# Two blocks on one core: factor transposes one product later in block one, both first low halves ahead of the upper transposes in block two

## The reference

```python
def reference(x, ...):
    x = first_block(x, ...)          # 2 layers
    return second_block(x, mem, ...) # 2 layers, then a last norm

# first_block, layer i
    xn = rmsnorm(h, norm_g[i])
    proj = xn @ w_in[i]              # hq, hf, hi, hgo, hz, nq, ... by columns
    log_f, k_hg = functions of sigmoid(hf)      # forget gate
    o_hg = hgrn2_chunkwise(hq, log_f, k_hg, hi) # 4 heads, a gated linear recurrence
    ...                              # a sparse attention from the other columns
    h = h + concat(y_hg, y_nsa) @ w_out[i]
    h = h + sigmoid(rmsnorm(h, ple_norm_g[i]) @ w_pg[i]) * (p[i] @ w_pp[i])

# second_block, layer l
    p = rmsnorm_2(x, norm_mix[l]) @ w_in[l]     # a_x, a_c, a_b, q, k, v, g, z, gates
    y_a = (a_b * conv3(a_c * a_x)) @ w_a_out[l] # short convolution
    ...                              # retention, spatial gating, gates
    x = x + merged @ w_o[l]
    x = x + cross_attention(rmsnorm_2(x, norm_xa[l]), rmsnorm_2(mem, norm_mem[l]), ...)
    h = rmsnorm_2(x, norm_ffn[l])
    x = x + (silu(h @ w1[l]) * (h @ w3[l])) @ w2[l]
```

## Time and profile before

| | |
|---|---|
| median of three runs | 2827.45 us (2824.11 to 2828.16) |
| span of the profiled execution | 2822.0 us |
| what lies around the span | the page gives no time of its own for the profiled execution; the three runs are 2.1 to 6.2 us above its span |
| TensorE busy | 2731.9 us (97%) |
| GpSimd, ScalarE, VectorE busy | 1385.1, 1271.7, 1176.7 us |
| granted TensorE clock, mean | 0.991 of full speed |
| instructions | 41633 |

### The profile page before, as it was taken

The page is one execution under the profiler, slowest core; times in us unless marked ns, Lnnn a source line. Parts: engine busy times, 40 slices in busy tenths (PEclk is TensorE's granted clock), DMA queues, the critical chain, the costliest instruction groups (busy, mean ns, idle before and its releaser), DMA issues.

```text
span 2822.0 us, 41633 instructions
## 1 busy us (share of the span) xinstructions
PE 2731.9 (97%) x13748; PEld 2286.9 (81%) x13748; DVE 1176.7 (42%) x2138; ACT 1271.7 (45%) x2187; POOL 1385.1 (49%) x1713
## 2 busy tenths in 40 slices
PE   8999899999999999999999999999999999999998
PEld 6889668788867878888888888888888788888887
DVE  4768752567775234422242321313442324242232
ACT  5554745655564543545443432424344544343233
POOL 4535444543544454454643655545455464365553
PEclk9999999999899999999999999999999999999999
DMA  5223113322301242233432333334223342233332
GB/s 152 72 51 87 26 31 90 87 72 57 92 9 45 83 113 70 83 102 100 120 98 60 110 100 90 97 97 114 70 82 101 96 125 90 65 107 102 93 97 97
DMA packets 270820, 242.47 MB, mean 86 GB/s; under 512 B 29376, under 2 KB 203648, under 8 KB 270592
## 3 DMA queue, kind: packets, MB, share of 16 engines
q1 hardware_dynamic: 267696, 235.12, 28.7%
q10 hardware_dynamic: 2896, 4.52, 0.5%
HBM read 237.51 MB, written 2.10 MB: 85 GB/s over the span
## 4 chain that ended last, share of the span: by engine, by line
PE 87%; DVE 5%; issue 4%; ACT 3%; POOL 0%; DMA 0%; DVEq 0%; ACTq 0%; POOLq 0%
PE bank L1988 11%; PE bank L1992 11%; PE bank L1991 11%; PE bank L1922 8%; PE bank L1925 8%; PE bank L1926 8%; PE bank L841 5%; PE bank L845 4%; PE bank L844 4%; PE bank L979 2%; PE bank L1877 2%; PE bank L891 1%; PE bank L827 1%; PE bank L894 1%; PE bank L895 1%
## 5 line engine op out<-in xcount | busy, mean ns | idle before, releaser
L2832 POOL TENSOR_TENSOR wlo<-raw,whi 128x256 fp32r<-128x256 f32 (+1 forms) x1616 | 1290.1, 830 | 1302.8 <-ACT whi L2137 1302.5
L2137 ACT CAST whi<-raw 128x1024 fp32r<-128x1024 f32 (+2 forms) x443 | 455.5, 1034 | 598.6 <-PE bank L1988 401.9
L1922 PE MATMUL bank<-xhi,whi 128*128 128x512 f32 x928 | 363.9, 392 | 1.6 <-DVE h L2524 1.6
L1926 PE MATMUL bank<-xhi,wlo 128*128 128x512 f32 x928 | 361.3, 389 | 0.0
L1925 PE MATMUL bank<-xlo,whi 128*128 128x512 f32 x928 | 361.1, 389 | 0.0
L1988 PE MATMUL bank<-whi,xhi 128*128 128x512 f32 x832 | 326.5, 392 | 3.9 <-DVE xlo L2415 3.9
L1992 PE MATMUL bank<-whi,xlo 128*128 128x512 f32 x832 | 324.0, 389 | 0.0
L1991 PE MATMUL bank<-wlo,xhi 128*128 128x512 f32 x832 | 323.8, 389 | 0.0
L841 PE MATMUL bank<-whi,xhi 128*128 128x512 f32 (+2 forms) x672 | 246.6, 367 | 5.5 <-DVE pT L1497 3.1
L844 PE MATMUL bank<-wlo,xhi 128*128 128x512 f32 (+2 forms) x672 | 242.2, 360 | 0.0
L845 PE MATMUL bank<-whi,xlo 128*128 128x512 f32 (+2 forms) x672 | 242.1, 360 | 0.0
(11 more groups left out here) (509 smaller groups left out, 4954.4 us busy)
## 6 DMA issues: line engine op xcount, KB each, us to landing
raw<-in_w_in SPq DMA_DIRECT2D x147, 512.0 KB, 3.7
raw<-in_w SPq DMA_DIRECT2D x132, 512.0 KB, 3.8
raw<-in_w_pg SPq DMA_DIRECT2D x16, 512.0 KB, 3.8
raw<-in_w_o SPq DMA_DIRECT2D x16, 512.0 KB, 3.8
raw<-in_xa_k SPq DMA_DIRECT2D x16, 512.0 KB, 3.9
raw<-in_xa_v SPq DMA_DIRECT2D x16, 512.0 KB, 3.8
raw<-in_xa_q SPq DMA_DIRECT2D x16, 512.0 KB, 4.0
raw<-in_xa_o SPq DMA_DIRECT2D x16, 512.0 KB, 3.8
```

The source lines that it names most:

```text
L1922: mm = pe.matmul(o, wh, rhs[0][:, k, :], start=(k == 0), stop=False)
L1926: mm = pe.matmul(o, wl, rhs[0][:, k, :], start=False, stop=(k == KD - 1))
L2137: nc.scalar.copy(whi[:, j % SLOTS, 0:nk * cols], raw[:, j % SLOTS, 0:nk * cols]).then_inc(hi_split, 1)
L2832: ins = nc.gpsimd.tensor_tensor(wlo[:, s, part], raw[:, s, part], whi[:, s, part].bitcast(F32), ALU.subtract)
```

## The change

Block one: the step `hf:0` is put ahead of `rows`, so on TensorE the four transposes of the factors come behind the product hf0 and not ahead of it. `sums_behind` puts the two back in their old order for DVE, which has to have the factors before it can scale hf0. Block two: the low half of ac0 is put ahead of `turn_high`, so that both low halves come first, and the high half of ax0 follows the transposes directly. No instruction is added or removed, and the order of the weight chunks stays.

```diff
@@ steps_one
     low = [("fm_low", *x) for x in hq[:3]]
-    s = low[:2] + [("turn_high", "mix")] + low[2:] + hq[:3] + [("sums", "mix")] + hq[3:] + [("rows", "mix")]
     hf = fm("hf", "w_in", 512, HG)
+    s = low[:2] + [("turn_high", "mix")] + low[2:] + hq[:3] + [("sums", "mix")] + hq[3:] + hf[:1] + [("rows", "mix")]
     early, late = ([(f"forget_{x}", hh) for hh in range(HG)] for x in ("early", "late"))
-    s += hf[:2] + early[:1] + hf[2:3] + early[1:2] + late[:1] + hf[3:] + early[2:3] + late[1:2]
+    s += hf[1:2] + early[:1] + hf[2:3] + early[1:2] + late[:1] + hf[3:] + early[2:3] + late[1:2]
@@ sums_behind
     out = list(steps)
+    i = out.index(("rows", "mix"))
+    out[i - 1:i + 1] = out[i], out[i - 1]
@@ steps_two
     low = [("fm_low", *x) for x in first]
-    s = low[:1] + [("turn_high", "mix")] + low[1:] + first + [("sums", "mix")] + g[:1] + [("rows", "mix")] + g[1:]
+    s = low + [("turn_high", "mix")] + first + [("sums", "mix")] + g[:1] + [("rows", "mix")] + g[1:]
```

## The result

| | before | changed |
|---|---|---|
| median | 2827.91 us (2824.11 to 2829.63, 14 runs) | 2831.67 us (2828.52 to 2837.55, 14 runs) |
| span of the profiled execution | 2822.0 us | 2830.5 us |
| granted TensorE clock in it | 0.991 | 0.986 |

The ratio is 1.0015, 95% interval 1.0008 to 1.0022: slower by some 4 us, where +0.3 was forecast. A change within 0.2% had been given 93%, and this one is. The median lies just inside the range, at its upper end, and it owes that to the width that was given for one fallen clock and for the spread of the medians, not to the sum. The interval doesn't reach down to the +0.3 of the sum (1.0001). The amount is that of rival (a), which had 12%.

A forecast was written before the change was run, and what follows sets the result against it. TensorE, busy 97% of the span, was taken to bound the kernel; block one -2.04, block two -0.18 and +2.53 sum to +0.31 us, so 2827.45 becomes 2827.8 us, range 2824.3 to 2831.8.

The forecast's parts named there:

- rival (a): Block two: clock falls behind the new stall in one or both executions, +2.8 or +5.3 us, 2830.3 to 2832.8; 12%.
- sums of stalls: Whole kernel: block one -2.04, block two -0.18 in its first execution and +2.53 in its second, together +0.31 us.
- forecast 1.02 each: Block one, each execution: the wait before the transposes of tD goes and hf1 begins earlier, gain 1.02 us.
- -0.18 as forecast: Block two, first execution: nearly all the 2.9 us stall moves behind the transposes; gain 0.18 us, bounds 0 to -0.4.
- forecast +2.53: Block two, second execution: ax0's high half waits exposed for the four turned tiles, +2.53 us, bounds +2.3 to +2.8.
- So I keep the whole gain: Block one: DVE's and ScalarE's chains start earlier too, so none of the 1.02 us per execution is given back.
- Rival (b): Block one: gain given back because the forget chain on ScalarE and DVE sets the attention's start; +2.35 us, 2829.8; 10%.
- the forecast -2.04: Block one, both executions: 1.02 us gained twice, -2.04 us, bounds -2.2 to 0.
- By the row at 988.4 I take no loss: Block two's new stalls: clock stays at 1.00 as behind the old stall; by another row each could cost 2.5 us.
- Rival (d): Both blocks: the change saves all it names, -4.9 us, 2822.5, needing the four tiles ready without cover; 3%.

The follow-up runs named there:

- the 4 matmuls: Block one's part alone, plus four idle 512-column matmuls (0.91 us) behind the factors' transposes in each execution: 2828.14 against 2827.73 us before, ratio 0.9999.
- the 9 matmuls: Block one's part alone, plus nine idle 512-column matmuls (2.05 us) behind the factors' transposes: 2832.71 against 2827.73 us before, ratio 1.0013.
- the filled kernel: Changed kernel plus ten idle 512-column matmuls behind block two's transposes of h: 2830.14 us, ratio 1.001 to before; repeated 2828.98 us, ratio 1.0003.
- the cover by g alone: Block one as before; in block two, ac0's low half early and g's first quarter behind h's transposes: 2824.53 us, ratio 0.9986 to before.

## Why the prediction was wrong

**Its sums of stalls were right.** Block one gains 0.90 and 0.94 us in the two rows of the table (forecast 1.02 each), and these stretches also hold what differs ahead of the change. Counted from the upper transposes (24.02 and 24.23 in the rows above), the first "decays" row comes after 69.04 or 69.05 us in all four traces that have block one as before, and after 67.93 to 67.99 in all eight that have its part: -1.08. In the second execution it is 69.66 to 70.11 against 68.58 to 69.13, on average -1.03. Block two's first execution: from its first transpose to a row 337 us later, 337.02 before and 336.84 changed, -0.18 as forecast. Its second: from the first matmul of ax0's low half to the first of its high half, 1900.63 to 1908.00 before and 1905.08 to 1914.79 changed, 7.37 against 9.71, that is +2.34 (forecast +2.53). At equal clock the changed kernel stands at +0.3, which was the forecast; that value rests on the correlation above.

**The step "So I keep the whole gain" failed.** The gain in block one is there at the places where it arises, and by the timed runs (-0.5 ± 0.5 in place of -2.04) 1.6 of its 2.0 us come back. Rival (b) had the amount, but not the mechanism: the chain of the forget gates does start the attention earlier (the first "decays" row is at 92.16, was 93.06). What the traces show in its place is the clock, in stretches of small products some 100 to 250 us later. In the second execution the distance from the first to the fourth "decays" row is 109.01 to 109.13 us in all five traces whose block one stands as before or has the 4 matmuls, and 109.91 to 111.15 in all eight that have block one's part; with the 9 matmuls it is 108.42. Behind it, up to the first transpose of block two, it is 308.15 in the first trace of block one's part alone and 304.21 with the 4 matmuls, so a single trace can lose more than the mean of the timed runs does. TensorE of block one's part alone, rows and windows:

```profile
574.40 0.65 PE L829 MATMUL bank<-ident,decays 128*128 128x128 f32 x4 [0.26 <-DVE decays L1638]
685.51 0.66 PE L829 MATMUL bank<-ident,decays 128*128 128x128 f32 x4 [0.61 <-DVE decays L1638]
```
```profile
669.00:675.00 6.00, 5.67 (x26) 5.68 (x27) 3.39 (x8) 2.20 (x5) 1.34 (x2) 0.50 0.00 1
754.00:771.00 17.00, 16.93 (x81) 16.53 (x81) 12.34 (x18) 9.09 (x16) 9.20 (x10) 0.51 0.60 178
```

And with the 4 matmuls:

```profile
576.91 0.65 PE L829 MATMUL bank<-ident,decays 128*128 128x128 f32 x4 [0.26 <-DVE decays L1640]
686.04 0.66 PE L829 MATMUL bank<-ident,decays 128*128 128x128 f32 x4 [0.61 <-DVE decays L1640]
```
```profile
670.00:676.00 6.00, 6.00 (x38) 5.84 (x39) 4.94 (x12) 2.07 (x4) 0.73 (x2) 0.72 0.03 11
755.00:770.00 15.00, 14.04 (x86) 13.64 (x85) 13.09 (x18) 9.83 (x17) 8.82 (x9) 0.66 0.64 185
```

The reader should see 111.11 against 109.13 us for the same work, and the clock at 0.50 for the whole of the first window in the one, at 0.72 in the other; in 754 to 771 it is 0.51 against 0.66. The first execution is less regular: from the fifth to the sixth of its "decays" rows, with the stretch around 270 to 298 in between, it takes 52.9 to 54.1 us in the five traces and 53.4 or 53.5 in five of the eight, but 57.4 or 57.5 in the other three, the changed kernel's first among them. The timed runs agree with the direction in their mean clock, 0.9886 before and 0.9877 with block one's part; the difference is 5.1 us more at the lower level, and at 0.28 each 1.4 us: most of the gap between -0.5 and the forecast -2.04. Four matmuls of no use bring the clock back to 0.9888, and cost -0.2 ± 0.8 us where 1.8 was added. That supports, at some 2.4 standard errors, that not the new order itself does harm but the shift in time of what follows; how a shift of 1 us moves a fall so far behind it no run shows. Which shifts are good could not be read from the traces ahead: 9 matmuls, a shift by 1 us the other way, stand at 0.9879 ± 0.0005 and cost 1.6 us more than the sum of stalls gives.

**The step "By the row at 988.4 I take no loss" failed, in the second execution alone.** Behind the new stall the clock fell in all three traces that have it open (the changed kernel twice, block two's part alone once), at 1916.00 in the window shown. From the first transpose to the last row of the table it takes 338.30 to 338.36 us there. With the stall filled it takes 336.73 and 336.75, in two of two traces. Windows and timeline of the filled kernel:

```profile
1910.03 1.91 PE L1879 MATMUL bank<-ident,h 128*128 128x128 f32 x16
1911.70 2.56 PE L1907 MATMUL bank<-xhi,whi 128*128 128x512 f32 x10
1914.17 0.50 PE L1927 MATMUL bank<-xhi,whi 128*128 128x512 f32 x1
```
```profile
1914.40:1919.00 4.60, 4.60 (x21) 3.77 (x21) 0.00 (x0) 2.58 (x3) 3.17 (x5) 1.00 0.24 91
```

The high half starts at 4.14 us from the first transpose in both, so the ten matmuls take nothing and give nothing but the clock, 1.6 us by these distances and 1.6 ± 0.8 by the times (3.25 less 1.64, from kernels that were not timed in one set); at equal clock the two kernels stand alike, at +0.3. Rival (a) thus came true in one execution of two, at 1.6 instead of 2.5. In the first execution the same stall (999.34, also 2.23 us) let the clock stand in three of three traces.

The error was to take one row of one execution as the rule. The old stall, at whose row I read a clock that held, makes it fall in four of six traces of kernels that have it. The kernel before, run again:

```profile
992.96 3.67 PE L1877 MATMUL bank<-ident,h 128*128 128x128 f32 x16 [2.88 <-DVE h L1587]
```
```profile
988.00:992.00 4.00, 2.07 (x10) 1.38 (x8) 2.70 (x5) 3.24 (x6) 0.00 (x0) 1.00 0.00 0
992.25:992.90 0.65, 0.00 (x0) 0.00 (x0) 0.65 (x2) 0.00 (x0) 0.00 (x0) 0.50 0.00 0
992.50:999.00 6.50, 6.04 (x23) 5.47 (x24) 3.49 (x6) 2.75 (x4) 0.00 (x0) 0.50 0.50 97
```

The stall is the same as in the earlier trace rows, 2.88 us, and the 16 transposes take 3.67 us and not 1.97. From them to the row 337 us on it takes 337.00 and 337.02 in two traces, and 338.39, 338.68 and twice 339.90 in four: 1.5 us more on average over the six. So the old stall cost more than its 2.9 us, and the change, which takes it away, should have gained that too. The Trainium skill, "TensorE: Matmul & The Clock Gate", Part 4 (PE-mode transpose), says that transposes don't count as activity for the clock as matmuls do. Three of three falls behind the new stall in the second execution agree with it, and so does the filled kernel, but the wait of 2.23 us alone could do the same: no run has this wait without the transposes ahead of it. The first execution, with the same stall and no fall, does not agree. At the old stall the transposes can't be the cause in the trace shown: the clock is at 0.50 from 992.25 on, while TensorE still stands.

**What isn't settled.** The terms found so far don't close the account. Stalls +0.3, block one's gain given back +1.6, the fall in the second execution +1.6 and the falls behind the old stall that go with it, -1.5, make +2.0, an estimate from the runs and distances above; +3.3 ± 0.5 was measured. The parts, -0.5 ± 0.5 and +1.1 ± 0.9, add to +0.7 ± 1.1, and the whole is +3.3 ± 0.5. The mean clock says it as well: 0.9877 and 0.9884 alone, 0.9868 together. That the second part shifts the rest of the kernel once more and so moves other falls would fit, but no run isolates it, and with these errors chance is not excluded.

**What removes it.** The stall itself is gone only when real work covers it. Timeline of the cover by g alone, TensorE, both executions:

```profile
991.84 1.97 PE L1877 MATMUL bank<-ident,h 128*128 128x128 f32 x16 [0.17 <-DVE h L1587]
994.06 0.50 PE L1988 MATMUL bank<-whi,xhi 128*128 128x512 f32 x1 [0.26 <-DVE xlo L2423]
...
1904.80 1.91 PE L1877 MATMUL bank<-ident,h 128*128 128x128 f32 x16
1906.97 0.50 PE L1988 MATMUL bank<-whi,xhi 128*128 128x512 f32 x1 [0.26 <-DVE xlo L2423]
```
```profile
1904.00:1910.00 6.00, 5.75 (x34) 4.80 (x33) 2.73 (x4) 2.42 (x4) 0.00 (x0) 1.00 0.69 181
```

Both the wait on h and the wait on xlo are 0.26 us or less, and TensorE is busy for 5.75 of 6.00 us at clock 1.00. This is what the change meant to reach: -4.0 us against before, and -7 against the changed kernel. The stalls alone give an estimate of -1.7 (2.2 saved in the first execution, 0.5 paid in the second, by distances to the row 337 us on); with the 1.5 for the falls behind the old stall it is -3.2, within the error of what was measured. Rival (d) came near this amount and needed the four tiles to be ready without cover; here a product that doesn't need them is the cover.

## What to carry to other kernels

Where an order puts two pieces of cover ahead of a handover, ask what covers the handover itself, in every execution of the loop: here the stall of one moved behind the transposes, and the other, which had none, got one; a product that needs neither side of the handover is what removes it. An edit of 1 us could not be booked at its own size here, where the clock falls in stretches behind it; to test that, put the time back with idle work and see whether it costs anything. One profiled execution doesn't say whether the clock holds behind a stall: read several before a price is put on it, or on its absence.

## What the hardware showed beyond expectation

The same stall is followed by clock 1.00 in one trace and 0.50 in another: in two and four of the six that have it, and in the kernel before in one of two. The mean clock of a run goes with some 60% of the variance of the times within a kernel. In the 113 runs of the kernel before that list it, it is 0.9886, which is 64 us of lower clock in 2829, or 18 us at 0.28 each (an estimate). The Trainium skill, "TensorE: Matmul & The Clock Gate", Part 1 (The HAM clock gate), says that the ramp at a kernel's start is run-variable and that its cost is under 1% of a typical span. The traces agree for the start: ten of fourteen have the clock at 0.50 from 16 to 20 us, as in the earlier trace rows, and four have it at 1.00. The start and all falls behind it together make the 18 us, 0.6% of the span; and what changes in them from one order of steps to another, 0.9893 to 0.9868 or some 14 us of lower clock and 4 us of time, is nearly as large as all the stalls that this change was about.

At the start of block two's second execution TensorE has an idle time that "issue" ends, 0.53 us in the trace after and 0.13 to 0.78 in twelve others; the trace before has none there. So 0.5 us of the 8.5 between the two traces is this. Block one's second execution begins with 0.26 to 0.50 us of it in six of fourteen traces, 0.50 in the one before. No run isolates its cause.
